# A hybrid trunk layer on one core: window attention's bias moved from TensorE to VectorE, and the mixers' attentions in a new order

## The reference

```python
a_q, a_k, a_v, b_a, b_g, c_q, c_kv, c_kr, d_u = split(rms_norm(x) @ w_in)
# window attention: 8 heads of 64, 2 key heads, window 128, with a bias by distance and a sink
logits = einsum(q, k) * 64**-0.5 + bias          # 128 queries against 256 keys (the first block: 128)
m = max(max(logits), sink); p = exp(logits - m)
o_a = (p / (sum(p) + exp(sink - m))) @ v
# convolution of width 31, layer norm, silu, pointwise product
o_b = silu(layer_norm(conv(a * sigmoid(g)))) @ pw_w + pw_b
# latent attention: 4 heads of 128 + 64 (rope); queries and keys from normed latents
logits = (q_nope @ k_nope + q_rope @ k_rope) * 192**-0.5   # causal
o_c = softmax(logits) @ v
# state space scan, gelu, gate
o_d = y * sigmoid(y @ glu_w + glu_b)
x = x + concat[rms_norm(o_a), rms_norm(o_b), rms_norm(o_c), rms_norm(o_d)] @ w_out
x = x + cross_attention(rms_norm(x), rms_norm(mem))        # 4 heads into 256 memory tokens
x = x + moe(rms_norm(x))                                   # 32 experts, top group, top 2 in it
```

## Time and profile before

| | |
|---|---|
| median of 3 runs | 1437.96 us (1437.96 to 1438.02) |
| the profiled execution | 1441.57 us, span of its instructions 1439.8 us |
| PE / DVE / ACT busy | 1223.4 / 606.5 / 221.5 us |
| mean granted TensorE clock | 0.919 of 2.4 GHz |
| read from HBM | 474.63 MB |

### The profile page before, as it was taken

The page is one execution under the profiler, slowest core; times in us unless marked ns, Lnnn a source line. Parts: engine busy times, 40 slices in busy tenths (PEclk is TensorE's granted clock), DMA queues, the critical chain, the costliest instruction groups (busy, mean ns, idle before and its releaser), DMA issues.

```text
span 1439.8 us, 16176 instructions
## 1 busy us (share of the span) xinstructions
PE 1223.4 (85%) x6745; PEld 573.4 (40%) x6745; DVE 606.5 (42%) x1291; ACT 221.5 (15%) x472; POOL 14.0 (1%) x31
## 2 busy tenths in 40 slices
PE   8999999999999999987677878787777777778786
PEld 5775564565885543232222222222222222222233
DVE  5989797678553452233122231222212221222222
ACT  3211032373012411101000100000000000000001
POOL 3000000000000000000000000000000000000000
PEclk9999999999999998999787998888899989888889
DMA  9333352622547579999999999999999999999998
GB/s 291 129 147 136 141 205 110 211 74 88 175 176 270 220 288 424 397 435 432 428 432 432 429 432 433 428 432 434 427 432 431 430 433 427 433 430 428 434 424 316
DMA packets 62728, 477.79 MB, mean 332 GB/s; under 512 B 13701, under 2 KB 21253, under 8 KB 45504
## 3 DMA queue, kind: packets, MB, share of 16 engines
q1 hardware_dynamic: 61392, 476.40, 80.2%
q0 software_dynamic: 864, 0.25, 0.2%
q10 hardware_dynamic: 400, 0.10, 0.0%
HBM read 474.63 MB, written 2.11 MB: 331 GB/s over the span
## 4 chain that ended last, share of the span: by engine, by line
PE 50%; DMA 33%; DVE 9%; ACT 4%; SPq 2%; issue 2%; DVEq 0%; ACTq 0%
DMA ring<-in_moe_w_up_dram 20%; DMA late_ring<-in_moe_w_up_dram 11%; PE bank L1284 11%; PE bank L732 11%; PE bank L1319 7%; PE bank L1049 5%; PE bank L1243 3%; PE bank L1305 3%; PE bank L1169 2%; PE bank L1040 2%; DMA ring<-in_moe_w_down_dram 1%; PE bank L1356 1%; SPq L501 1%; PE bank L1125 1%; PE bank L746 1%
## 5 line engine op out<-in xcount | busy, mean ns | idle before, releaser
L1284 PE MATMUL bank<-ring,x_gathered 128*32 128x512 f32 x1184 | 250.1, 672 | 49.9 <-DMA late_ring<-in_moe_w_up_dram 35.9
L1284 PE MATMUL bank<-late_ring,x_gathered 128*32 128x512 f32 x800 | 202.7, 683 | 43.2 <-DMA ring<-in_moe_w_up_dram 41.9
L2697 DVE TENSOR_TENSOR tokens_out<-tokens_out,bank 128x512 f32<-128x512 f32 x240 | 148.5, 681 | 194.9 <-PE bank L1356 194.9
L732 PE MATMUL bank<-ring,hT 128*128 128x512 f32 (+2 forms) x416 | 156.0, 536 | 3.3 <-ACT hT L1556 1.7
L2680 DVE SCALAR_TENSOR_TENSOR hidden<-hidden,bank 128x128 f32<-128x128 f32 x31 | 8.9, 288 | 346.0 <-ACT hidden L1877 346.0
L1243 PE MATMUL bank<-x_tok,select 128*32 128x512 f32 x512 | 115.9, 1033 | 7.3 <-DVE select L2589 4.2
L1284 PEld LDWEIGHTS bank<-ring,x_gathered 128*32 128x32 f32 x1184 | 66.5, 122 | 139.7 <-issue 137.7
L732 PEld LDWEIGHTS bank<-ring,hT 128*128 128x128 f32 x416 | 78.6, 190 | 77.9 <-issue 67.0
L1319 PE MATMUL bank<-ring,hidden 128*32 128x512 f32 x560 | 87.8, 783 | 18.2 <-DVE hidden L2682 18.2
L1284 PEld LDWEIGHTS bank<-late_ring,x_gathered 128*32 128x32 f32 x800 | 52.6, 124 | 115.1 <-issue 110.7
L1356 PE MATMUL bank<-y_slots,weight_slots 32*128 32x512 f32 x496 | 72.1, 651 | 29.5 <-ACT y_slots L1892 21.7
(11 more groups left out here) (459 smaller groups left out, 1266.2 us busy)
## 6 DMA issues: line engine op xcount, KB each, us to landing
ring<-in_moe_w_up_dram SPq DMA_DIRECT2D x19, 4096.0 KB, 40.4
ring<-in_moe_w_down_dram SPq DMA_DIRECT2D x16, 4096.0 KB, 29.9
ring<-in_moe_w_gate_dram SPq DMA_DIRECT2D x16, 4096.0 KB, 39.2
late_ring<-in_moe_w_down_dram SPq DMA_DIRECT2D x13, 4096.0 KB, 29.1
late_ring<-in_moe_w_gate_dram SPq DMA_DIRECT2D x12, 4096.0 KB, 38.9
late_ring<-in_moe_w_up_dram SPq DMA_DIRECT2D x10, 4096.0 KB, 39.2
ring<-in_w_in_dram SPq DMA_DIRECT2D x20, 1024.0 KB, 8.2
ring<-in_w_out_dram SPq DMA_DIRECT2D x16, 1024.0 KB, 6.1
```

Of the source, the lines that this page charges most:

```text
L732: mm = pe.matmul(b, lhs(i)[:, P * tt:P * tt + P], piece_view(key)[:, c, at:at + cols], start=i == 0, stop=i == n - 1)
L1284: mm = pe.matmul(gu_bank[SLOTS * c:SLOTS * c + SLOTS, :], XGT[:, at, n % 4, n // 4, :], pieces[c % 2][:, FF * (n % 8):FF * (n % 8) + FF], ...
L2697: ins = v.tensor_tensor(y, x, mix[c][:, :], ALU.add)
```

## The change

- **Bias.** The `flip` products go. PE writes only the scores; DVE adds the bias band as it reads the bank (`add_bias`). Since the band's rows are reversed, the queries are transposed in reverse order, and the probabilities are turned back when ACT copies them (`backwards`). Latent scores too are read from the bank by DVE, scaled and masked in one step, and ACT has no copy to make.
- **Pairs.** Window scores go to two banks in turn, an even head and an odd one, so that neighbouring products use rows 0 to 63 and 64 to 127. The rope parts of latent queries and keys are laid out on two row halves (`turned_pairs`: products with the identity in place of transposes), and the narrow products of two heads follow each other. Window outputs alternate between column halves.
- **Order of PE.** `xk0` and `xk1` move behind the latents' dense products and behind the latent scores. Latent attention comes ahead of window attention; its softmax stands beside `xk1`, the window softmax beside the first products into `w_out` (`wq0` and the new `wq1`, each with two groups). `kxT` moves behind the folded products. The order of the groups in `w_out` becomes 3, 1, 2, 0.
- **Order of DVE and ACT.** The gelu comes ahead of the centring of the convolution, and its tanh ahead of the drain of `xv1`. The norm of the memory keys moves into the folded products, ACT's drains of `kxT` ahead of those of `cT0`. The parts of `drain_parts` no longer wait for each other.
- **Loads.** `wqb`, `glu`, `pw`, `wkvb` come ahead of `xk`; the bias band follows `wkvb`. `skv`'s last two pieces wait for half of `sq1` (`half_used`). Four warm-up products instead of twelve at the start; `token_rows(1)` behind the second tile's drains.

The diff, cut to its core:

```diff
...
-    t += ["xv0", "xv1", "cm", "xk0", "cv", "cqT0", "cqT1", "ckvT", "xk1"]
-    t += ["mq00", "mq10", "mq01", "mq11", "glu0", "glu1", "sqT0", "sqT1", "skT", "mkv00", "mkv01", "mkv10", "mkv11"]
-    t += ["pw0", "pw1", "gs3", "sl00", "sl01", "sl10", "sl11", "gs1", "sl12", "sl13", "sp00", "sp01"]
-    t += ["qnT0", "qnT1", "qrT0", "qrT1", "knT0", "knT1", "krT", "so0", "kxT0", "kxT1", "ml0", "ml10", "ml11"]
-    t += ["sp10", "sp11", "sp12", "sp13", "wq0", "so1", "mp0", "mp10", "mp11", "mo0", "mo1", "gs0", "gs2"]
+    t += ["xv0", "xv1", "cm", "cqT0", "cqT1", "ckvT", "mq00", "mq10", "cv", "mq01", "mq11", "glu0", "glu1", "pw0", "pw1"]
+    t += ["mkv00", "mkv01", "mkv10", "mkv11", "gs3", "gs1", "xk0", "qnT0", "qnT1", "qrT0", "qrT1", "knT0", "knT1", "krT"]
+    t += ["ml00", "ml01", "ml10", "ml11", "sqT0", "sqT1", "skT", "xk1"]
+    t += ["sl00", "sl01", "sl10", "sl12", "sl11", "sl13", "mp0", "mp10", "mp11", "wq0", "mo0", "mo1", "wq1", "gs2"]
+    t += ["sp00", "sp01", "sp10", "sp11", "sp12", "sp13", "so0", "so1", "gs0"]
     t += [f"wo{n}{part}" for n in range(4) for part in ("abcd" if n in SEVEN else "01")]
+    t += ["kxT0", "kxT1"]
...
-WO_ORDER = (3, 1, 0, 2)
+WO_ORDER = (3, 1, 2, 0)
...
 def piece_order():
...
+    w += [("wqb", 0), ("wqb", 1), ("glu", 0), ("pw", 0), ("wkvb", 0)]
     w += [("xk", q) for q in range(4)]
-    w += [("glu", 0), ("wqb", 0), ("wqb", 1), ("wkvb", 0), ("pw", 0)]
...
+                    if g in ("za", "sq") and q < 2:
+                        sp.wait_ge(s["half_used"], 1 if g == "za" else 2)
                     elif g == "wo0" and q in WO_ORDER[0:2]:
+                        wait_filled(sp, "wq1")
...
+            def window_scores(n, names, firsts):
...
                 w = P * (n + 1)
...
+                count = 4 if n == 0 else 2
+                banks = [fill(name) for name in names]
+                for i in range(count):
+                    for b, first in zip(banks, firsts):
+                        h = HEAD_AT[first + i]
+                        r = slice(64 * (h % 2), 64 * (h % 2) + 64)
+                        mm = pe.matmul(b[:, w * i:w * i + w], SQT[r, h // 2, P * n:P * n + P], SKT[r, h // 4, 0:w],
+                                       start=True, stop=True)
+                        if i == count - 1:
+                            filled(mm)
             def window_output(n, probs):
                 b = fill(f"so{n}")
...
+                for i in range(SWA_H // 2):
                     for kb in range(n + 1):
+                        for at in (i, SWA_H // 2 + i):
+                            h = HEAD_AT[at]
+                            o = b[64 * (h % 2):64 * (h % 2) + 64, P * (h // 2):P * (h // 2) + P]
+                            a = P * (at * (n + 1) + kb)
+                            mm = pe.matmul(o, SKV[:, kb, P + 64 * (h // 4):P + 64 * (h // 4) + 64], probs[:, a:a + P],
+                                           start=kb == 0, stop=kb == n)
...
+            def turned_pairs(name, src):
+                b = fill(name, cols=2 * P)
+                for i in range(2):
+                    for d in range(2):
+                        mm = pe.matmul(b[64 * d:64 * d + 64, P * i:P * i + P], src(i, d), ident, start=True, stop=True)
...
             wait_task(pe, "cqT1")
-            for g in range(2):
-                for tt in range(TT):
-                    latent_query(tt, g)
+            for tt in range(TT):
+                latent_query(tt, 0)
+            pe.wait_ge(s["conv_sq"], 1)
+            row_sum("cv", RG[:, 0, :])
+            for tt in range(TT):
+                latent_query(tt, 1)
...
+            pe.wait_ge(s["og_sq"], 1)
+            row_sum("gs3", SUM3)
+            pe.wait_ge(s["og_sq"], 2)
+            row_sum("gs1", SUM1)
+            memory_product("xk", 0)
+            pe.wait_ge(s["mq_n"], 1)
+            key_turned("qnT", lambda tt: [MQ[:, tt, QK_D * h:QK_D * h + NOPE] for h in range(MLA_H)])
+            for tt in range(TT):
+                turned_pairs(f"qrT{tt}", lambda i, d: MQ[:, tt, QK_D * (2 * i + d) + NOPE:QK_D * (2 * i + d) + QK_D])
+            pe.wait_ge(s["mkv_n"], 1)
+            key_turned("knT", lambda tt: [MKV[:, tt, 256 * h:256 * h + NOPE] for h in range(MLA_H)])
+            turned_pairs("krT", lambda tt, d: CKV[:, tt, 256:320])
...
+            def latent_scores(n):
+                w = P * (n + 1)
+                q = slice(P * n, P * n + P)
+                banks = [fill(f"ml{n}{i}", cols=2 * w) for i in range(2)]
+                for i in range(2):
+                    for b, h in zip(banks, (2 * i, 2 * i + 1)):
+                        pe.matmul(b[:, w * i:w * i + w], QNT[:, h, q], KNT[:, h, 0:w], start=True, stop=False)
+                    for b, r in zip(banks, (slice(0, 64), slice(64, 128))):
+                        mm = pe.matmul(b[:, w * i:w * i + w], QRT[r, i, q], KRT[r, 0:w], start=False, stop=True)
+                        if i == 1:
+                            filled(mm)
...
+            memory_product("xk", 1)
+            wait_task(pe, "skT")
+            window_scores(0, ("sl00", "sl01"), (0, 4))
...
+            pe.wait_ge(s["ml_p"], 1)
+            transposes("mp0", [L0[:, P * h:P * h + P] for h in range(4)])
+            pe.wait_ge(s["ml_p"], 2)
+            for i in range(2):
+                transposes(f"mp1{i}", [L0[:, 512 * (i + 1) + P * k:512 * (i + 1) + P * k + P] for k in range(4)])
+            filled(mix_out(0, 0, (0, 1), fill("wq0"), True, True))
+            wait_task(pe, "mp0")
+            latent_output(0)
+            wait_task(pe, "mp11")
+            latent_output(1)
+            filled(mix_out(0, 1, (0, 1), fill("wq1"), True, True))
+            pe.wait_ge(s["og_sq"], 3)
+            column_sums("gs2", SQ2)
+            pe.wait_ge(s["sl_p"], 1)
+            for i in range(2):
+                transposes(f"sp0{i}", [SL0[:, 512 * i + P * k:512 * i + P * k + P] for k in range(4)])
+            pe.wait_ge(s["sl_p"], 2)
+            for i in range(4):
+                transposes(f"sp1{i}", [SL1[:, 512 * i + P * k:512 * i + P * k + P] for k in range(4)])
+            wait_task(pe, "sp01")
+            window_output(0, PT0)
+            wait_task(pe, "sp13")
+            window_output(1, PT1)
...
+            mix_out(0, 0, (2,), reserved("wo00"), True, False)
             pe.wait_ge(s["og_sq"], 4)
+            row_sum("gs0", SUM0)
+            mix_out(0, 1, (2,), reserved("wo01"), True, False)
+            filled(mix_out(0, 0, (3,), fill("wo00"), False, True))
...
+                transposes(f"kxT{tt}", [KX[:, tt, P * h:P * h + P] for h in range(XA_H)])
...
+            act.wait_ge(s["gelu_in"], 1)
+            st.link(nc.scalar.activation(L0[:, 0:1024], L0[:, 0:1024], ACT.Tanh, scale=0.7978845608028654), "gelu_th")
...
+            for tt in range(TT):
+                drain(f"mq{tt}0", MQ[:, tt, 0:384], cols=384)
+            root_mean_square("cv", RG[:, 1, :])
+            for tt in range(TT):
+                drain(f"mq{tt}1", MQ[:, tt, 384:768], cols=384)
             act.wait_ge(s["conv_y"], 1)
             st.link(nc.scalar.activation(SQG, ZT, ACT.Tanh, scale=0.5), "conv_th")
...
+            root_mean_square("gs1", RG2[:, 1, :])
+            drain("xk0", KX[:, 0, :], scale=MROWS[:, 0:1])
...
+            drain("krT", KRT[:, :], cols=T)
             act.wait_ge(s["ml_max"], 1)
             exps(L0[:, 0:512], 4, P, 0, "ml_exp")
             act.wait_ge(s["ml_max"], 2)
             exps(L0[:, 512:1536], 4, T, 4, "ml_exp")
...
+            skip("ml00", "ml01", "ml10", "ml11")
...
+            def backwards(b):
+                return four(4)(b)[:, :, ::-1]
+            for tt in range(TT):
+                drain(f"sqT{tt}", SQT[:, :, P * tt:P * tt + P], backwards, scale=SM[:, 152:153])
...
+            drain("xk1", KX[:, 1, :], scale=MROWS[:, 1:2])
+            for n, scores in enumerate((SL0, SL1)):
+                act.wait_ge(s["sink_in"], n + 1)
+                st.link(nc.scalar.activation(SM[:, 256 + 8 * n:264 + 8 * n], SM[:, 256 + 8 * n:264 + 8 * n], ACT.Exp))
+                exps(scores, 8, P * (n + 1), 8 * n, "sl_exp")
+                if n == 0:
+                    skip("sl00", "sl01", "sl10", "sl12", "sl11", "sl13")
+                    wait_turn(act, "mp0")
+                    drain("mp0", PT[:, 0:512])
+                    drain("mp10", PT[:, 512:1024])
+                    drain("mp11", PT[:, 1024:1536])
+            skip("wq0")
+            wait_turn(act, "mo0")
             drain("mo0", OT[:, 8:12, 0:P], four(4))
             drain("mo1", OT[:, 8:12, P:T], four(4))
+            skip("wq1")
+            wait_turn(act, "gs2")
+            root_mean_square("gs2", RG2[:, 2, :])
+            for i in range(2):
+                drain(f"sp0{i}", four(4)(PT0[:, 512 * i:512 * i + 512]), backwards)
+            for i in range(4):
+                drain(f"sp1{i}", four(4)(PT1[:, 512 * i:512 * i + 512]), backwards)
...
-            wait_turn(act, "cT00")
+            wait_turn(act, "kxT0")
```

(61 more changed lines are left out.)

243 lines of the change are left out of this document (52 added, 191 removed).

## The result

The changed kernel took 1445.81 us (median of 20 runs, 1443.08 to 1447.71), the one before 1442.24 in the same comparison; the ratio is **1.0027**, 95% interval 1.0014 to 1.0040. On the 1437.96 us from which the forecast counts that is 1441.8, 3.9 us slower, where the forecast was 1438.1; it lies above the forecast's own range (1439.4) and 0.3 above the end of the wider one (1441.5). The 3.6 us that I took off for the profiled execution are not shown to be the profiler's: the 20 runs of the kernel before spread from 1436.53 to 1448.29, with 1441.57 among them. The forecast difference of +0.1 us does not depend on this.

What follows compares the result with a forecast made beforehand. PE was taken to bound the changed stage, DVE and ACT taking over up to gs1. Folded products −2.8, key drains +1.3, clock +1.6 made +0.1 us: 1438.1, own range 1436.5 to 1439.4, eight in ten 1432.4 to 1441.5.

Steps and rivals of the forecast that it cites:

- PE work that goes: Attentions: bias products dropped (6.3 us), paired scores and outputs shorter, memory-key transposes moved; about 15.3 us less PE work.
- The waits: PE waits 4.8 us ahead of the latent queries, 1.8 and 2.8 at gs3 and gs1, 1.1 and 2.6 in the tail.
- DVE's walk to gs1: DVE's work from the convolution through gelu, norms and squares, worked out to let PE do gs1 at 275.75 us.
- the 5 us gap: PE's 4.8 us wait ahead of the latent queries; its 1.6 us clock cost was to be swallowed by the `cv` wait.
- Ahead of the attentions: Earlier `skv` load and unlinked ACT drains bring `xv0` to 202.9 instead of 204.58; the missing warm-up products change nothing.
- Moved on: Key drains ahead of the `cT0` drains on ACT delay PE's first query product by 1.26 us; other moved work is hidden.
- TensorE's clock: Slow clock after PE's waits: 1.6 us on the path behind gs3 and gs1, bounds 0 and 2.9.
- the tail's wait of 2.6: PE's wait for DVE's `group_scale(0)` before the last two groups; clock cost priced at nothing, up to 1.6 us.
- the row of 2.0 us: Profile row of the kernel before: after 2.0 us idle the clock stayed at 1.00; used against a fall in the tail.
- slower: the clock: Rival: clock stays low longer at gs1 (2.9 instead of 1.6) and falls again in the tail (1.6); 1441.0 us, chance 0.17.

Runs made afterwards that it cites:

- the joined run: Changed kernel plus four edits: first memory-key product earlier, gelu tanh later, window group's scaling ahead of weight sums, key drains behind cT0; ratio 0.9927 to the kernel before.

## Why the prediction was wrong

- **PE work that goes**: right. Window scores 2.9, latent scores 5.5; the bias products measured 6.0 of the 6.3 priced (by the rows two of the six took 0.95 to the next start, which makes 6.1). What the pairs give lies in the latent scores (2.8); for the window scores the mere two halves are nearly enough.
- **The waits**: right for the five long ones, within 0.3 us, and DVE and ACT do take over as said. DVE's walk to gs1 holds: 275.65 with the waits filled, 275.75 worked out. That the changed kernel has 277.20 is the clock's doing, 1.0 at y0 and 0.5 behind the 5 us gap. What the walk lacked are the 0.26 and 0.86 ahead of the window outputs; without the falls the folded products start 1.5 us earlier than in the kernel before (362.35 against 363.83), not 2.8.
- **Ahead of the attentions**: that the 8 missing warm-up products cost and give nothing is borne out by the run with twelve (1.0029, the changed kernel 1.0027). What the sum lacked is the wait at y0's second half, 3.25 instead of 2.01, with a fall of the clock behind it. Without that fall xv0 starts at 202.46, with it at 203.50; I had said 202.9.
- **Moved on**: right; 1.15 measured for 1.26.
- **TensorE's clock**: this is the step that failed. I put one fall of 1.6 in the sum, behind the waits at gs3 and gs1, and that one measured 1.7. But the tail's wait of 2.6 was priced at "nothing, up to 1.6", by the row of 2.0 us that left the clock at 1.00, and its fall cost 1.7; the fall at the 5 us gap was to be swallowed by the wait for `cv`, and 0.5 of it reached gs1; the one at y0 had no term at all and cost 1.0. In place of 1.6 the runs show some 5 us (4.9 in the trace, 4.7 in the medians, 5.3 in the ratios, with the intervals given above). The row of 2.0 us covers the idle time itself; that the clock held behind it is seen in the products of 1.09 and 2.12 us there, and it is one trace of a single wait, which could not settle the tail's two.
- So the outcome is the rival "slower: the clock", which I gave 0.17 and 1441.0; 1441.8 lies 0.8 above it. That its 4.5 for the clock comes so near the 4.9 is partly luck: it had 2.9 at gs1, where 1.7 was measured, and nothing at y0 and behind the 5 us gap. The Trainium skill (TensorE: Matmul & The Clock Gate, What's actually happening) says that the slow clock is the default state and activity lifts it; the four slow stretches behind waits agree. My reading of it, that every new wait is paid twice, does not hold: 1.16 at the tail left 1.00, and behind the same waits of about 1.05 and 2.35 the clock fell in seven traces (8.80) and stayed up in two (7.11, the run with the first memory product ahead and the one with the bias products). What decides between these is not settled here.

## What to carry to other kernels

A new wait of a dense engine has two prices: its own length and the slow stretch behind it, here 1.7 us for waits of 2.35 and 2.48, so count nearly double unless a trace shows that it isn't, and fill it with real work first and with overwritten products if there is none. Work saved on the bounding engine is worth only what the engines beside it can follow: work out each wait that takes its place, then look for a dense product that needs nothing of them and put it there. A gap whose removal gains nothing alone can be worth some 4 us once the next one is closed, as in the joined run, so edits of one chain are judged together.

## What the runs showed of the hardware

- A wait of 2.35 us, with one of about 1.05 ahead of it, was followed by a slow stretch in seven traces and by none in two. A wait of 1.69 ahead of the latent scores was followed by one in the joined run (2.07 for 1.13), and one of 1.68 at the same place by none in the run with only the memory product moved. The length of a wait alone does not tell.
- Narrow products on two row halves need no strict turns: window scores took 3.44 when four, then two of a half followed each other, 2.89 in turns, and outputs on two column halves 2.02 and 1.97.
- A table load of 1.28 us ahead of a root held up nothing where it ended before the product that the root needs (244.22), and came onto DVE's path where the products ahead of it ran at the slow clock (7.96 for 5.43): DVE waited 3.28 there instead of 1.37.
